# Two transformer blocks on one core: RMS norms whose inverse is applied behind the product, squares on GpSimd, products that share a turning set of banks

## The reference

```
# block one, two layers
for l in range(2):
    h = rms_norm(x, attn_norm[l])              # x * rsqrt(mean(x*x) + 1e-6) * gain
    proj = h @ w_in[l]                         # 1024 -> 2762
    ... three kinds of attention over slices of proj ...
    x = x + concat(o_fox, o_diff, o_dsa) @ w_out[l]
    h = rms_norm(x, ffn_norm[l])
    gate, up = split(h @ w_gate_up[l])         # 2 x 2816
    x = x + (silu(gate) * up) @ w_down[l]
# block two: for each of two layers, for x and for the context
    mod = silu(c) @ ada_w[l] + ada_b[l]        # shift, scale, gate: 3 x 1024
    u = rms_norm(h, norm_g[l]) * (1 + scale) + shift
    y = mixer(u); h = h + gate * y             # layer 0: window + latent attention, layer 1: grid
out = rms_norm(h, final_g)
```

## Time and profile before

| what | value |
|---|---|
| median of 3 runs | 2731.34 us |
| profiled execution, its span | 2735.1 us, 2733.3 us |
| TensorE matmuls busy | 2412.1 us, 88% |
| VectorE / ScalarE / GpSimd busy | 46% / 36% / 5% |
| mean granted TensorE clock | 0.938 |
| matmuls of the products of layer 0 | 45.8 to 188.4 in-product, 400.0 to 443.3 out, 457.1 to 701.0 gate and up, 703.4 to 823.3 down |
| layer 1 | 837.6 to 978.4 in-product, 1180.9 to 1227.5 out, 1241.3 to 1485.3 gate and up, 1487.6 to 1609.0 down |
| block two | 1609 to 2733 |

### The profile page before, as it was taken

The page is one execution under the profiler, slowest core; times in us unless marked ns, Lnnn a source line. Parts: engine busy times, 40 slices in busy tenths (PEclk is TensorE's granted clock), DMA queues, the critical chain, the costliest instruction groups (busy, mean ns, idle before and its releaser), DMA issues. The chain is left out here.

```text
span 2733.3 us, 33353 instructions
## 1 busy us (share of the span) xinstructions
PE 2412.1 (88%) x13113; PEld 1898.6 (69%) x13113; DVE 1255.8 (46%) x1761; ACT 976.5 (36%) x1566; POOL 137.9 (5%) x98
## 2 busy tenths in 40 slices
PE   5986988999998948898999978987999969998987
PEld 3873666888786835576887857866677747886666
DVE  4766834333218767534333225316555351225653
ACT  2133663334213236634342122223454232115551
POOL 0001110000000021100000000000000000001210
PEclk8986899999999978999999998998999989999999
DMA  4520002322224410011322221211000113213311
GB/s 156 204 89 1 1 13 67 107 92 92 93 92 172 148 46 1 1 62 63 106 92 92 95 67 44 66 71 58 15 16 13 49 54 115 77 62 53 53 22 47
DMA packets 137945, 189.07 MB, mean 69 GB/s; under 512 B 37077, under 2 KB 88274, under 8 KB 137810
## 3 DMA queue, kind: packets, MB, share of 16 engines
q1 hardware_dynamic: 102610, 168.55, 18.4%
q10 hardware_dynamic: 35216, 18.88, 2.9%
HBM read 179.94 MB, written 7.47 MB: 69 GB/s over the span
## 5 line engine op out<-in xcount | busy, mean ns | idle before, releaser
L458 DVE TENSOR_TENSOR w_low<-w_raw,w_high 128x2048 fp32r<-128x2048 f32 (+3 forms) x140 | 304.4, 2175 | 697.6 <-ACT w_high L453 694.9
L453 ACT ACTIVATE w_high<-w_raw 128x2048 fp32r<-128x2048 f32 (+3 forms) x140 | 255.0, 1822 | 785.4 <-PE ps L469 720.9
L469 PE MATMUL ps<-h_hi,w_high 128*128 128x512 f32 x976 | 375.3, 385 | 42.4 <-DVE h_lo L1041 30.3
L469 PE MATMUL ps<-h_lo,w_high 128*128 128x512 f32 x976 | 372.4, 382 | 0.0
L469 PE MATMUL ps<-h_hi,w_low 128*128 128x512 f32 x976 | 372.1, 381 | 0.0
L469 PE MATMUL ps<-w_high,h_hi 128*128 128x512 f32 (+2 forms) x736 | 284.9, 387 | 36.4 <-DVE h_lo L1041 27.5
L469 PE MATMUL ps<-w_high,h_lo 128*128 128x512 f32 (+2 forms) x736 | 281.2, 382 | 0.0
L469 PE MATMUL ps<-w_low,h_hi 128*128 128x512 f32 (+2 forms) x736 | 280.7, 381 | 0.0
L469 PEld LDWEIGHTS ps<-h_hi,w_high 128*128 128x128 f32 x976 | 185.7, 190 | 87.0 <-issue 31.0
L469 PEld LDWEIGHTS ps<-h_hi,w_low 128*128 128x128 f32 x976 | 185.5, 190 | 35.2
L469 PEld LDWEIGHTS ps<-h_lo,w_high 128*128 128x128 f32 x976 | 186.1, 191 | 33.8
(11 more groups left out here) (276 smaller groups left out, 3661.3 us busy)
## 6 DMA issues: line engine op xcount, KB each, us to landing
w_raw<-in_w_gate_up SPq DMA_DIRECT2D x44, 1024.0 KB, 4.9
w_raw<-in_w_in SPq DMA_DIRECT2D x20, 1024.0 KB, 5.6
ada_w<-in_ada_w SPq DMA_DIRECT2D x16, 1280.0 KB, 5.6
w_raw<-in_w_down SPq DMA_DIRECT2D x20, 1024.0 KB, 4.9
w_raw<-in_c_in_w SPq DMA_DIRECT2D x16, 1024.0 KB, 5.5
w_raw<-in_w_out SPq DMA_DIRECT2D x8, 1024.0 KB, 4.9
w_raw<-in_ab_in_w SPq DMA_DIRECT2D x8, 1024.0 KB, 5.0
bias<-bias_scratch ACTq DMA_DIRECT2D x32, 224.0 KB, 5.2
```

Source lines behind the costliest of these rows:

```text
L453: e.activation(w_high[j % 2][:, 0:size], w_raw[j % 2][:, 0:size], ACT.Copy).then_inc(sig.w_high_done, 1)
L458: e.tensor_tensor(w_low[j % 2][:, 0:size], w_raw[j % 2][:, 0:size], w_high[j % 2][:, 0:size].bitcast(F32), ALU.subtract).then_inc(sig.w_lo ...
L469: mm = e.matmul(dst, lhs, rhs, start=start and a == 0, stop=stop and a == 2)
```

## The change

**Norms of block one.** `Norm` is replaced by `Gained` there. x times gain, without the inverse, is split into h1_hi and h1_lo: ScalarE forms the high part with the gain as its scale, VectorE the low part in one fused operation. Both run chunk by chunk behind the evictions of the product before (`AddOut(follow=...)`), or behind the first copies of x. GpSimd squares each chunk and adds it to square_sum. TensorE sums square_sum over partitions once: for the in-product into one column for each 128 tokens, for the gate product into a whole bank. The root and the reciprocal follow, and the inverse is applied on eviction: in `RowsOut` as a scale per partition in the copies to proj, in `GatedOut` as a multiplication of the gate bank on VectorE before the silu, and one of the silu's result on GpSimd after it.

```
+ class Gained(Stage):
+     chase = True
+     def scalar(...):
+         for k in range(KD):
+             e.wait_ge(sig.evac_vec, B["evac_vec"] - KD + k + 1)
+             e.activation(h1_hi[:, k, :], x_t[:, k, :], ACT.Copy, scale=self.gain(k))
+             if self.opens and k == 3: cut_high(e, B, 0, self.size)
+         cut_high(e, B, 1, self.size)
+     def cut_chunk(self, e, B, k):                       # VectorE, called by AddOut and Start
+         e.wait_ge(sig.part_high, ...)
+         e.scalar_tensor_tensor(out=h1_lo[:, k, :], in0=x_t[:, k, :], scalar=self.gain(k),
+                                in1=h1_hi[:, k, :].bitcast(F32), op0=ALU.mult, op1=ALU.subtract)
+     def gpsimd(...):
+         for k in range(KD):
+             dst = square_sum[:] if k == 0 else self.squares_[:, k % 2, :]
+             e.tensor_tensor(dst, x_t[:, k, :], x_t[:, k, :], ALU.mult)
+             if k:
+                 e.wait_ge(sig.sq_ready, B["sq_ready"] + k + 1)
+                 e.tensor_tensor(square_sum[:], square_sum[:], self.squares_[:, k % 2, :], ALU.add)
```

```
+ # GatedOut.vector, then .scalar, then .gpsimd
+ e.tensor_tensor(gated[:, m, :], ps[:, st.bank(i, m), :], inv_wide[:], ALU.mult)
+ e.activation(gated[:, m, :], gated[:, m, :], ACT.Silu)
+ e.tensor_tensor(gated[:, m, :], gated[:, m, :], inv_wide[:], ALU.mult)
```

**In-product.** One product of six groups (five of 512 columns, one of 202), not looped. Each carries 4 tiles of the conditioning (a 128x512 slice of ada_w). VectorE keeps the sum for v = 0 and does it after both weight cuts; GpSimd has v = 1, in two operations a chunk, each behind a wait for the one before:

```
+ elif v == 0:
+     ins = e.scalar_tensor_tensor(out=acc, in0=w, scalar=c, in1=acc, op0=ALU.mult, op1=ALU.add)
+ else:
+     ch.step(e.tensor_scalar(ada_tmp[:], w, c, None, ALU.mult))
+     ch.wait(e)
+     ins = e.tensor_tensor(acc, acc, ada_tmp[:], ALU.add)
```

More of the change, by code:

```diff
@@ L169, in wait @@
     def wait(self, e):
-        if not (isinstance(self.n, int) and self.n == 1):
+        if self.n != 1:
             e.wait_ge(self.sem, self.n)
[L173 to L183, removed]
 def build_program(nc, I, consts, out):
@@ L509, in __init__, with taken_banks, bank, spots @@
                 self.counts["pair"] = self.pieces * groups // 2
-                assert self.pieces * groups % 2 == 0 and (self.pieces % 2 == 0 or loop == 0)
+                assert self.pieces * groups % 2 == 0
+            def taken_banks(self):
+                return self.groups * self.all_banks
+            def bank(self, i, n):
+                return (self.first_bank + i * self.all_banks + n) % self.ring
             def order(self):
                 for m in range(self.tiles):
-                    yield m, m, 0, self.tokens
                     if self.spill:
[L517 to L541, removed]
+                        yield 2 * m, m, 0, S
+                        yield 2 * m + 1, m, S, self.tokens - S
+                    else:
+                        yield m, m, 0, self.tokens
+            def spots(self, i, nk):
+                tiles = list(self.order())
+                if self.paced and i == 0:
+                    return [(t, kk) for kk in range(nk) for t in tiles]
+                return [(t, kk) for t in tiles for kk in range(nk)]
+            def columns(self, i):
+                return self.width
+            def each(self, B):
+                for i in range(self.groups):
                     b = B.at(self.per, i)
@@ L580, in vector, with beside @@
-                self.each(e, B, ch, body)
+                for b, i, odd in self.each(B):
+                    self.cuts(e, b, i, odd, cut_low)
+                    self.evac.vector(e, b, L, self, i, ch)
+            def beside(self, e, B, L, i, j, n):
+                pass
             def tensor(self, e, B, L, ch):
-                start = B
-                def body(e, B, i, odd):
-                    k0 = self.k_at
+                for b, i, odd in self.each(B):
+                    k0, width = self.k_at, self.columns(i)
@@ new lines, in tensor, with scalar, take_condition @@
+            def tensor(self, e, B, L, ch):
+                Product.tensor(self, e, B, L, ch)
+                self.sum_condition(e, B.at(self.per, self.groups - 1), self.groups - 1)
+            def scalar(self, e, B, L, ch):
+                for b, i, odd in self.each(B):
+                    self.cuts(e, b, i, odd, cut_high)
+                    if i == 0:
+                        self.norm.root_rows(e, b)
+                    self.evac.scalar(e, b, L, self, i, ch)
+            def take_condition(self, e, B, L, i):
@@ L824, in tensor, with vector, gpsimd @@
+            def vector(self, e, B, L, ch):
+                for b, i, odd in self.each(B):
+                    self.cuts(e, b, i, odd, cut_low)
+                    if i == 0:
+                        self.norm.invert_wide(e, b)
+                    self.evac.vector(e, b, L, self, i, ch)
+            def gpsimd(self, e, B, L, ch):
+                for b, i, odd in self.each(B):
+                    self.evac.gpsimd(e, b, L, self, i, ch)
             def tensor(self, e, B, L, ch):
-                start = B
```

707 lines of the change are left out of this document (403 added, 304 removed).

## The result

The changed kernel takes 2754.4 us, the median of 4 runs (2750.69 to 2755.97), beside 2731.45 (2728.57 to 2737.35) for the kernel before: a ratio of 1.0079, 95% interval 1.0065 to 1.0093. It is 23 us slower. The forecast was 2700 in a range of 2640 to 2732, so both time and direction were wrong. The profiled execution has a span of 2754.0 us against 2733.3.

What follows compares the result with a forecast made beforehand. TensorE's matmuls take 88% of the span; only lower-clock matmuls and TensorE's waits cost time. Terms 5 - 8 + 12.8 + 4.8 + 15.3 = 29.9 us off 2731.3 gave 2701, stated as 2700, range 2640 to 2732.

Steps and rivals of the forecast that it cites:

- In-product and conditioning: Block one's in-products: GpSimd multiplication 0.61 us, chain 22.5 us a group; layer 1 loses 8, layer 0 gains 5.
- Rival 2: In-product: GpSimd bounds it if a multiplication by a column costs 1.27 us; 2764 us, chance 0.12.
- rival 3: Whole kernel: gains and losses cancel, at about 0.9 us per multiplication or through stalls lowering the clock; 2731, chance 0.10.
- Start: Layer 0's start: transposes near 12.0, first product matmul near 24 instead of 45.77, 21.8 us early, 17 given back later.
- Squares on GpSimd: Block one's norms: squares and adds take 17.9 us, or 26.2 when run in turn with VectorE's work; 26.2 taken.
- Rival 1: GpSimd and VectorE: sharing costs little, squares take 17.9 us and matmuls bound a group; 2634 us, chance 0.17.
- Ffn norms: Two norms before gate products: 13.8 us falls to 7.4, a wait of 6.5 plus 0.9; gain 6.4 each, 12.8 together.
- Down product: Both layers' down product: no longer waits 2.39 us for the last act_lo; gain 4.8.
- Block two: Joined products with turning banks lose waits of 12.3 us, and tile order gives 3; together 15.3, bounds 9 and 20.
- the tile order: Block two's paced first products: each chunk runs over all tiles, removing waits for h_lo; 3 us in one, 0 in the other.

Runs made afterwards that it cites:

- the one with the cheaper form: The changed kernel with GpSimd's multiplication by a column written as a two-input operation with the column broadcast along the row: 2734.8 us in one run.
- the best kernel: Changed kernel with sums on VectorE, squares on ScalarE, bank 1, earlier ada load, sixth group's own cut then sum first, constants loaded behind weights: 2646.2 us, ratio 0.9674.

## Why the prediction was wrong

- **In-product and conditioning: this step failed, by one term.** It said "the nearest is GpSimd's copy of the same width, 0.61, with one input like it", and took 0.61 for a range of 0.61 to 1.27. Alone it takes 1.58, above the upper end, and 2.05 in place. The chain of a group was put at 22.5 us and took 27.1 in layer 1; six groups are 162.6 us from the first product to the last add for 135, and these 28 us are the difference between the 8 lost in the forecast and the 38.4 measured, but for 3. The price alone would have made 46 us more in six groups; sharing, put at 7.2 us a group, was about 4.4 (27.1 less the 22.7 of the prices alone with their gaps), and gives 17 back. Layer 0 fell short by 31, and 26 of them are the same chain (160.7 us for 135). The bound was wrong in kind: the number of inputs isn't what orders these prices, since the square and the spread product have two and take 1.04, and two different tensors take 1.27, all below 1.58.
- **Rival 2 was the right mechanism.** It said GpSimd bounds the in-product from 0.92 us per multiplication on, and with 1.27 gave 2764; the result is 2754. The experiment with the sum back on VectorE (2696) and the one with the cheaper form (2735) show it from two sides. That its number comes so near is partly luck: it has a price too low (1.27 for 1.58) and sharing too high (7.2 for 4.4 a group), and a chain of 27.8 us for the 27.1 measured. It had a chance of 0.12, for a price with no row of its own that enters the sum 96 times; everything else was worth 38 us, and by the forecast's own sum 0.3 us more on this price turns the sign. Of rival 3, the part that new stalls bring the lower clock back is seen too: 0.84 for 0.94 in layer 1's stage, some 6 us.
- **Start.** "First product matmul near 24" was 33.80. Two causes, both shown: the constants on another queue delay the vectors (transposes at 16.48 instead of 12.0; 12.48 when they go behind the weights), and bank 0 is claimed before its last chunk is copied (4.4 us). VectorE's cut of piece 0 took 2.98 beside GpSimd for 2.29. None of it counted for the result, since layer 0 then waits for GpSimd.
- **Squares on GpSimd.** The sharing was right: the product of squares 1.04 alone, 1.59 in place, the add 1.27 and 1.58 to 1.74, and VectorE's low part 0.74 and 1.1. Rival 1 is out. The whole chain was put at 26.2 us and took 24.6 in both ffn norms, 22.8 in layer 1's in-product and 26.9 in layer 0's.
- **Ffn norms.** A wait of 6.5 was forecast, 8.04 and 8.05 measured, and the sum behind it holds the next product matmul back by 1.05 (1300.35 to 1301.40) for 0.9. The chain of squares was shorter than forecast, but in layer 0 it began 5.0 us behind the begin of the out product's last piece and not 2.1: VectorE's cut of the next weights, 2.29 us from 453.45 on, stands ahead of the first eviction, and the forecast left it out there. With the down product's wait the forecast gain was 17.6, and 22.2 was measured. The mechanism held and the size was somewhat better. What the forecast did not weigh was that ScalarE and VectorE had the room for the squares themselves.
- **Down product.** It begins with no wait, as forecast.
- **Block two.** 15.3 forecast inside 9 to 20, 22.0 measured. Joining the products gives 17 of it by their own lengths; the tile order, put at 3 in the first products, gives nothing there and 2.7 in the latent product. That a wait costs more than its length, by the matmuls at the lower clock behind it, was the missing part.
- **What would show it wrong.** The test named was the stretch from the down product's end to layer 1's last condition sum, wrong over 175 us. It is 192.3. The other sign, a multiplication mean over 0.9 for rival 2, stood at 2.05.
- **Not foreseen: the narrow group.** Even on VectorE, the sixth group's sum of 11.1 us has no wide product to hide behind. The forecast had its length ("the sixth as long as the others") but only as a part of GpSimd's chain. It costs 12 to 13 us in each layer with both sums on VectorE.

## What to carry to other kernels

A price that no row shows and that enters the sum 96 times has to be measured, or its whole range has to decide the forecast. "One input" was no reason to take the lower end. Work moved to an idle engine is free only if its whole chain for a group, with the time that it holds VectorE and is held by it, stays under the group's matmuls: at 27.1 against 23.6 us GpSimd, idle before, became the bound, and the best kernel has taken this work off it again. Short last groups need their side work moved ahead, and only the side work: look at what else the moved call holds.

## What the runs showed of the hardware

- GpSimd, 128x512 in float32, alone: copy 0.61, square 1.04, product with a column spread over the row 1.045, add of two tensors 1.26, product of two different tensors 1.27 to 1.30 (in the kernels), a tensor by a constant 1.49, a tensor by a column 1.58 us. The spread product does the same work as the last in two thirds of the time.
- Beside VectorE the multiplication by a column took 2.43 us in the mean, and 1.57 where VectorE ran nothing; one that met a weight cut took 3.48.
- VectorE's fused operation with two SBUF inputs shares with GpSimd, too (0.742 alone, 1.105 beside the squares). The copies of x out of PSUM do not show it: 0.69 before, 0.68 beside GpSimd.
- The same attention stage was 191.8 us at a granted clock of 0.86 in one kernel and 196.2 at 0.82 in the next, whose in-product was 5 us shorter. That the shorter in-product brought the lower clock is not shown: the four executions of that kernel alone lie at 2644 to 2658 us, with mean granted clocks of 0.950 to 0.942. Over all profiled executions this stage lies at 191.4 to 199.8 us, which is as large as most single edits here, so their worth is best read from their own stage, and from the whole only with several runs.
